# Sample states by head pair of four samples instead of by group of one sample, in the Mamba-2 part of a hybrid decoder step

## The reference, cut to what matters

```
new_state[b,h,p,n] = exp(sum of dt*a over the 4 tokens) * h0[b,h,p,n]
                     + sum_t  decay_to_end[t,h] * dt[t,h] * x[t,h,p] * B[t,g,n]
y_off[t,h,p]       = exp(acs[t,h]) * sum_n  C[t,g,n] * h0[b,h,p,n]
```

## Time and profile before

| | us |
|---|---|
| median of 3 runs | 2291.16 (2288.71 to 2292.43) |
| profiled execution | 2290.49 |
| its span | 2289.3 |
| TensorE busy | 2222.1 |
| sample states: first turn to the end of the turns in `carry` | 1308.18 to 1361.33 |

### The profile page before, as it was taken

One profiled execution on the slowest core, in us unless ns is written; L12 is line 12 of the kernel. 1 busy time (PEld: TensorE's weight loads), 2 busy tenths in 40 slices (PEclk: granted clock), 3 DMA queues, 4 the chain that ended last, 5 costly groups with the idle time before them and its releaser, 6 DMA issues.

```text
span 2289.3 us, 41851 instructions
## 1 busy us (share of the span) xinstructions
PE 2222.1 (97%) x16986; PEld 2161.8 (94%) x16986; DVE 1193.4 (52%) x1545; ACT 820.4 (36%) x798; POOL 162.5 (7%) x224
## 2 busy tenths in 40 slices
PE   6999999999999999999899899899999999999998
PEld 6999999999999999988787879899999999999997
DVE  5545445454455557556436656555544555445554
ACT  5333333332333343344353434433323333333333
POOL 2410000000000130100000402000000000000022
PEclk8999999999999999999999999999999999999999
DMA  8665565655656567656875465665566665666552
GB/s 197 171 166 158 162 176 161 168 155 163 177 158 169 145 160 208 186 168 190 268 227 174 126 176 154 166 168 160 164 167 166 166 164 159 172 166 166 158 156 95
DMA packets 696130, 386.51 MB, mean 169 GB/s; under 512 B 18216, under 2 KB 677836, under 8 KB 695192
## 3 DMA queue, kind: packets, MB, share of 16 engines
q1 hardware_dynamic: 691528, 378.79, 60.1%
q0 software_dynamic: 4112, 5.94, 1.0%
q10 hardware_dynamic: 384, 0.30, 0.0%
HBM read 373.86 MB, written 11.13 MB: 168 GB/s over the span
## 4 chain that ended last, share of the span: by engine, by line
PE 87%; DVE 5%; SPq 2%; ACT 2%; issue 2%; DMA 1%; POOL 0%; ACTq 0%; DVEq 0%; POOLq 0%
PE bank L785 28%; PE bank L787 27%; PE bank L786 27%; DVE wlo L1507 1%; SPq L476 1%; PE bank L810 1%; ACT whi L1192 1%; SPq L475 1%; PE bank L1067 1%; PE bank L983 0%; DVE lseg L1870 0%; DMA kpage<-cache_k 0%; PE bank L1074 0%; DVE xn_lo L1497 0%; PE bank L929 0%
## 5 line engine op out<-in xcount | busy, mean ns | idle before, releaser
L785 PE MATMUL bank<-xn_hi,whi 128*128 128x288 f32 x3536 | 1059.0, 299 | 29.5 <-DVE wlo L1507 11.5
L786 PE MATMUL bank<-xn_hi,wlo 128*128 128x288 f32 x3536 | 1050.5, 297 | 0.0
L787 PE MATMUL bank<-xn_lo,whi 128*128 128x288 f32 x3536 | 1046.8, 296 | 0.0
L1507 DVE TENSOR_TENSOR wlo<-wraw,whi 128x2048 fp32r<-128x2048 f32 (+3 forms) x341 | 726.4, 2130 | 401.4 <-ACT whi L1192 401.0
L1192 ACT CAST whi<-wraw 128x2048 fp32r<-128x2048 f32 (+3 forms) x341 | 604.8, 1775 | 748.9 <-PE bank L787 743.5
L785 PEld LDWEIGHTS bank<-xn_hi,whi 128*128 128x128 f32 x3536 | 670.1, 190 | 39.9 <-issue 20.5
L787 PEld LDWEIGHTS bank<-xn_lo,whi 128*128 128x128 f32 x3536 | 673.0, 190 | 0.0
L786 PEld LDWEIGHTS bank<-xn_hi,wlo 128*128 128x128 f32 x3536 | 671.3, 190 | 0.1
L786 PE MATMUL bank<-h_hi,wlo 128*128 128x288 f32 x1376 | 407.1, 296 | 0.0
L787 PE MATMUL bank<-h_lo,whi 128*128 128x288 f32 x1376 | 406.6, 296 | 0.0
L785 PE MATMUL bank<-h_hi,whi 128*128 128x288 f32 x1376 | 401.8, 292 | 0.0
(11 more groups left out here) (351 smaller groups left out, 1149.2 us busy)
## 6 DMA issues: line engine op xcount, KB each, us to landing
wraw<-ffn_w_gate SPq DMA_DIRECT2D x86, 1024.0 KB, 5.9
wraw<-ffn_w_up SPq DMA_DIRECT2D x86, 1024.0 KB, 5.8
wraw<-ffn_w_down SPq DMA_DIRECT2D x64, 960.0 KB, 5.5
wraw<-w_in SPq DMA_DIRECT2D x40, 1024.0 KB, 6.4
wraw<-ffn_w_down SPq DMA_DIRECT2D x32, 832.0 KB, 5.2
kpage<-cache_k SPq DMA_DIRECT2D x64, 256.0 KB, 3.0
vpages<-cache_v SPq DMA_DIRECT2D x64, 256.0 KB, 3.5
wraw<-w_out SPq DMA_DIRECT2D x64, 256.0 KB, 3.1
```

What stands on the lines that cost most here:

```text
L785: pe.matmul(out, hi, rhs_hi, start=k == 0, stop=False)
L786: pe.matmul(out, lo, rhs_hi, start=False, stop=False)
L787: return pe.matmul(out, hi, rhs_lo, start=False, stop=k == nk - 1)
L1507: dve.tensor_tensor(tile_ap(wlo, s, nk), tile_ap(wraw, (base + j) % LOADS, nk), tile_ap(whi, s, nk).bitcast(F32), ALU.subtract).then_inc(s ...
```

## The change

- A unit becomes one head pair c = u//2 of four samples b0 = 4*(u%2) to b0+3, [128, 4 samples, 128]. `h0_of` gives the new view of the states; the number of units, their size and the ring stay.
- The outer product of a unit is one product of 512 columns: weights `xsn` of the pair, moving operand `bexp` with B of the group copied for each of four samples and masked to that sample's tokens. `bexp` for all samples and both groups is made once, in `decay_x`, in two instructions; it lies in a part of `xn_hi` that is free then.
- The C products of a unit are four products of 128 columns, one for each sample, on the four column tiles of the array, in every unit. Each column tile (row group of 32 in PSUM) collects its samples' rows; two units of a pair accumulate.
- `carry` scales all 128 rows, and the eight turns become eight products with `stack` (four identities one above the other), which add the four row groups while turning.
- The scaled sample x lies at rows 32 to 63 (`SX`) of `xsn`, and `nat_e` must stand in all four row groups: `turn_copies` makes such copies with products against the identity on several column tiles.
- `bmask` is made on VectorE instead of GpSimd, at the start, with `stack`.

```diff
-    bexp = Plan(nc, AT["lseg"], A1)("bexp", [P, 4, 256])
+    bexp = Plan(nc, AT["xn_hi"] + 4 * 4 * N, AT["xn_lo"])("bexp", [2 * NS, 2, ND, P])
+    SX = slice(NS, 2 * NS)
...
-        return t[0, u // 2, 8 * (u % 2):8 * (u % 2) + 8].rearrange("(j e) p n -> (e p) j n", e=2)
+        return t[0, 4 * (u % 2):4 * (u % 2) + 4, u // 2 * 2:u // 2 * 2 + 2].rearrange("b e p n -> (e p) b n")
+
+    def copies(ap, n):
+        return ap.unsqueeze(1).to_broadcast([ap.shape[0], n, ap.shape[1]])
+
+    def copied_rows(b):
+        return P if b < 2 else 2 * NS
...
-        pool.memset(bmask[:], 1.0).then_inc(sem("pool_fill"), 1)
...
-        pool.affine_select(out=bmask[:], in_=bmask[:], compare_op=ALU.is_ge, fill=0.0, base=0, pattern=[[-NT, ND]],
-                           channel_multiplier=1).then_inc(sem("pool_fill"), 1)
...
-        pool.affine_select(out=bmask[:], in_=bmask[:], compare_op=ALU.is_ge, fill=0.0, base=NT - 1,
-                           pattern=[[NT, ND]], channel_multiplier=-1)
...
+            def turn_copies(out, src, many, n=P):
+
+                if many == 1:
+                    return turn(out, src, n)
+                for r in range(many):
+                    m = pe.matmul(out[r * NS:(r + 1) * NS, :], src, ident[0:n, 0:n], start=True, stop=True)
+                return m
...
-                            turn(to[0:rows_of(b), b * 144 + pl * 48:b * 144 + pl * 48 + 48], sc48[0:48, pl, toks(b)], 48)
-                    turn(to[0:NS, 432:480], e48[0:48, :], 48).then_inc(side_done("nat"), 1)
+                            src = sc48[0:48, pl, toks(b)]
+                            turn_copies(to[:, b * 144 + pl * 48:b * 144 + pl * 48 + 48], src, 1 if b < 2 else 2, 48)
+                    turn_copies(to[:, 432:480], e48[0:48, :], 4, 48).then_inc(side_done("nat"), 1)
...
-                            m = turn(to[0:rows_of(i), c * P:(c + 1) * P], xsT[:, 4 * half + c, toks(i)])
+                            src = xsT[:, 4 * half + c, toks(i)]
+                            m = turn_copies(to[:, c * P:(c + 1) * P], src, 1 if i < 2 else 2)
...
-                        b, g = (i - 1) // 2, (i - 1) % 2
-                        to = claim(pe, "up", i - 1)
-                        pe.wait_ge(sem("bexp_ready"), b + 1)
-                        for j in range(4):
-                            c = 4 * g + j
-                            m = pe.matmul(to[:, j * P:(j + 1) * P], xsn[0:NS, 2, c * P:(c + 1) * P],
-                                          bexp[0:NS, b % 4, g * ST:(g + 1) * ST], start=True, stop=True)
-                        m.then_inc(side_done("up", i - 1), 1)
-                        if g == 1:
-                            for q in range(2):
-                                copied(pe, "ht", 2 * b + q)
-                            for q in range(2):
-                                pe.matmul(bank[2 + q][NS * q:NS * (q + 1), :], cpad[:, q, b, :], h0t[:, q, :],
-                                          start=b == 0, stop=b == ND - 1).then_inc(sem("h0t_used"), 1)
+                        u = i - 1
+                        c, b0 = u // 2, 4 * (u % 2)
+                        to = claim(pe, "up", u)
+                        pe.wait_ge(sem("bexp_ready"), 2)
+                        pe.matmul(to[:, :], xsn[SX, 2, c * P:(c + 1) * P], bexp[SX, c // 4, b0:b0 + 4, :],
+                                  start=True, stop=True).then_inc(side_done("up", u), 1)
+                        copied(pe, "ht", u)
+                        for q in range(4):
+                            m = pe.matmul(bank[2 + c // 4][NS * q:NS * (q + 1), c % 4 * P:(c % 4 + 1) * P],
+                                          cpad[:, c // 4, b0 + q, :], h0t[:, u % 2, q * P:(q + 1) * P],
+                                          start=b0 == 0, stop=b0 > 0)
+                        m.then_inc(sem("h0t_used"), 1)
...
-                        m = turn(to[:, j * NS:(j + 1) * NS], ys[0:NS, j * P:(j + 1) * P], NS)
+                        m = pe.matmul(to[:, j * NS:(j + 1) * NS], ys[:, j * P:(j + 1) * P], stack[:], start=True, stop=True)
...
+        dve.tensor_reduce(stack[:], ident[:].rearrange("p (r t) -> p t r", t=NS), AX.X, ALU.add)
+        dve.tensor_reduce(bmask[SX, :], ident[SX, SX].rearrange("p (b t) -> p b t", t=NT), AX.X, ALU.add)
...
-                    for b in range(3):
-                        n = rows_of(b)
-                        xv = xsn[0:n, b, :].rearrange("p (h c) -> p h c", c=HD)
-                        m = dve.tensor_tensor(xv, xv, spread(nat[0:n, b, 96 + 32:96 + 48], HD), ALU.mult)
+                    for b, rows in ((0, slice(0, P)), (1, slice(0, P)), (2, SX)):
+                        xv = xsn[rows, b, :].rearrange("p (h c) -> p h c", c=HD)
+                        m = dve.tensor_tensor(xv, xv, spread(nat[rows, b, 96 + 32:96 + 48], HD), ALU.mult)
                     m.then_inc(sem("xw_ready"), 1)
+                    for g in range(2):
+                        dve.tensor_tensor(bexp[SX, g, :, :], copies(bnat[SX, 2, g * ST:(g + 1) * ST], ND),
+                                          spread(bmask[SX, :], ST), ALU.mult).then_inc(sem("bexp_ready"), 1)
                 elif what == "unit":
-                    if i % 2 == 0 and i < 2 * ND:
-                        b = i // 2
-                        if b >= 4:
-                            take(dve, "up", 2 * (b - 4) + 1)
-                        dve.tensor_scalar(bexp[0:NS, b % 4, :], bnat[0:NS, 2, :], bmask[:, b:b + 1], None, ALU.mult)\
-                            .then_inc(sem("bexp_ready"), 1)
...
-                                                         scalar=dec[:, 4 * g + j, b:b + 1], in1=src[:, cs],
+                                                         scalar=dec[:, u // 2, 4 * (u % 2) + j:4 * (u % 2) + j + 1],
+                                                         in1=src[:, cs],
...
-                        dve.tensor_tensor(ys[0:NS, g * 512:(g + 1) * 512].rearrange("p (h c) -> p h c", c=HD),
-                                          bank[2 + g][NS * g:NS * (g + 1), :].rearrange("p (h c) -> p h c", c=HD),
-                                          spread(nat_e[0:NS, 32 + 8 * g:40 + 8 * g], HD), ALU.mult).then_inc(sem("ys_ready"), 1)
+                        dve.tensor_tensor(ys[:, g * 512:(g + 1) * 512].rearrange("p (h c) -> p h c", c=HD),
+                                          bank[2 + g][:, :].rearrange("p (h c) -> p h c", c=HD),
+                                          spread(nat_e[:, 32 + 8 * g:40 + 8 * g], HD), ALU.mult).then_inc(sem("ys_ready"), 1)
```

More of the change, by code:

```diff
@@ L100, in build @@
     hot = fixed("hot", [P, H_SSD], F32R)
+    stack = fixed("stack", [P, NS])
+    bmask = fixed("bmask", [2 * NS, ND])
     mseg3 = fixed("mseg3", [P, 3 * P + NS])
@@ L578, in _ @@
         pool.memset(col[:], 0.0).then_inc(sem("pool_fill"), 1)
-        pool.wait_ge(sem("pool_fill"), 6)
+        pool.wait_ge(sem("pool_fill"), 5)
         for c in (0, 2):
@@ L585, in _ @@
                            channel_multiplier=1).then_inc(sem("pool_fill"), 1)
-        pool.affine_select(out=bmask[:], in_=bmask[:], compare_op=ALU.is_ge, fill=0.0, base=0, pattern=[[-NT, ND]],
-                           channel_multiplier=1).then_inc(sem("pool_fill"), 1)
         pool.affine_select(out=head_rows[:], in_=head_rows[:], compare_op=ALU.is_ge, fill=0.0, base=0, pattern=[[1, NS]],
                            channel_multiplier=-NT).then_inc(sem("pool_fill"), 1)
-        pool.wait_ge(sem("pool_fill"), 9)
+        pool.wait_ge(sem("pool_fill"), 7)
         pool.affine_select(out=head_rows[:], in_=head_rows[:], compare_op=ALU.is_ge, fill=0.0, base=NT - 1,
@@ L599, in _ @@
         pool.memset(col[0:72, 0:1], -1.0).then_inc(sem("pool_fill"), 1)
-        pool.wait_ge(sem("pool_fill"), 10)
+        pool.wait_ge(sem("pool_fill"), 8)
         pool.memset(col[SR, 0:1], 1.0).then_inc(sem("tables_ready"), 1)
@@ L1024, in mix_tensor @@
                     for c in range(2):
-                        m = turn(to[0:rows_of(i), c * P:(c + 1) * P], xsT[:, 8 + c, toks(i)])
+                        src = xsT[:, 8 + c, toks(i)]
+                        m = turn_copies(to[:, c * P:(c + 1) * P], src, 1 if i < 2 else 2)
                     m.then_inc(side_done("b", i), 1)
@@ L1728, in mix_vector @@
                     dve.tensor_copy(nat[:, 0:2, :].rearrange("p b c -> p (b c)"), src[:, 0:288])
-                    dve.tensor_copy(nat_e[0:NS, :], src[0:NS, 432:480])
-                    dve.tensor_copy(nat[0:NS, 2, :], src[0:NS, 288:432]).then_inc(side_read("nat"), 1)
+                    dve.tensor_copy(nat_e[:], src[:, 432:480])
+                    dve.tensor_copy(nat[0:2 * NS, 2, :], src[0:2 * NS, 288:432]).then_inc(side_read("nat"), 1)
                     src = take(dve, "dec")
@@ L1836, in mix_vector @@
                 elif what == "turn_x":
-                    n = rows_of(i)
+                    n = copied_rows(i)
                     for half in range(2):
@@ L1845, in mix_vector @@
```

(2 more changed lines are left out.)

2 lines of the change are left out of this document (removed).

## The result

The changed kernel takes 2292.99 us (median of 12 runs, 2291.18 to 2299.74) against 2289.2 (12 runs, 2284.2 to 2294.27): ratio 1.0022, interval 1.0013 to 1.0031. The difference of 3.8 us is small, but the whole interval lies above 1: the change made the kernel slower. The forecast was 0.8 us faster.

The account below looks back on a forecast made before the run. TensorE, busy for 97% of the span, bounds the kernel. Saved 4.4 us less 3.6 lost is 0.8 net: the profiled 2290.49 becomes 2289.7, as median of runs 2290.4; range 2286 to 2296, same verdict at 0.75.

Parts of the forecast that it names:

- the first one: Opening step: TensorE is busy for 97% of the span, so the question is which of its stretches the change touches.
- Rival 2: Old-state loads bind at three places with longest landing: 2293.7; with falls of TensorE's clock 2298.5, slower; chance 0.09.
- Outer product: Sample-state units: one 512-column product takes 0.97 us (bounds 0.85 to 0.98) instead of 1.085; 1.8 us saved.
- C products: Sample-state units: four 128-wide products on four column tiles take 0.35 us per unit (0.24 to 0.40); 1.6 us saved.
- rival 1: Four column tiles don't run at once when a unit brings one group: 9.4 us more, 2299.8, slower; chance 0.05.
- Wait for ScalarE: Sample-state units: TensorE's 0.26 us wait for ScalarE's copy of the turned state goes four times; 1.0 us saved.
- Old states: Late loads stall the turns of states 6, 10 and 14 by 0.4 us each, 1.2 in all; 0.9 lost.
- carry: Eight turns become eight products, 16 passes, taking 1.8 us in place of 0.5; 1.3 us lost (up to 1.65).
- The clock's one fall in the stage: Sample-state stage before the change: TensorE's clock fell once, around 1340; a mean of 0.97 means 1.6 us lost.
- rival 4: The one fall of TensorE's clock in the sample-state stage goes: 1.6 us faster, 2288.8; chance within the forecast's 0.75.
- Turns with copies and gates: Before `scores`, sample turns of x and B: 0.95 us lost (0 to 1.2); gate turns: 0.45 lost (0.2 to 0.6).

Follow-up runs that it names:

- a_pad96: Changed kernel with 96 unused bytes behind bmask, so h_hi and h_lo start 256 bytes later than in the kernel before: 2289.6 us, ratio 0.9996.
- a_out4: a_pad96 with the one 512 wide outer product of a unit put back to four of 128 columns: 2293.86 us (one run).
- a_fill: a_pad96 with output tiles from carry on moved one place forward, so a tile of products stands before carry: 2287.48 us, ratio 0.9995.
- b_pad160: Kernel before the change with 160 unused bytes behind hot, nothing else: 2295.62 us, ratio 1.0026.
- b_xn32: Kernel before the change with 32 unused bytes in front of xn_hi and 32 more behind hot: 2296.24 us, ratio 1.0025.
- a_xn96: Changed kernel with gaps of 224 bytes in front of xn_hi and 128 in front of xn_lo: 2280.35 us (6 runs), ratio 0.9966.
- a_w32: Changed kernel with 32 bytes in front of the split weights and 96 behind them: 2276.79 us (6 runs), ratio 0.9952.

## Why the prediction was wrong

The forecast, 2290.4 with same as the likeliest, missed: the kernel got slower by 3.8 us, and not a little faster. The range, 2286 to 2296, holds the 2292.99 all the same, and 3.8 is less than the 4.6 that the prediction took for the least that can be told. For the changed stages in sum the forecast is not refuted: `a_pad96` differs from before by -0.04%, the forecast by -0.03%. But the interval of `a_pad96` is 0.12% to either side, and the terms below are off in both directions, so that the agreement is in part luck.

**The step that failed** is the first one: "the question is which of its stretches the change touches", answered by the stages whose code changed. The two new tiles of the fixed region, 160 bytes, were costed only by what fills them. They also move every tile behind them, and so touch 4128 products of the down projections: a loss of 4.7 us, the largest single effect that the runs show. No rival had this. Rival 2's 2293.7 lies near the measured time, by another mechanism, and its mechanism was not there: no turn of an old state waits for its load in the changed kernel's trace.

The single terms, by their own names:

- **Outer product**: mis-sized. 1.05, not 0.97; outside my bounds (0.85 to 0.98). 16 x 0.035 = 0.6 saved, not 1.8. On top of the stream of 0.85 lie 0.20, not the 0.13 that the C products before the change had; why, no run shows.
- **C products**: 0.36, as forecast (0.35). Four tiles do run at once; rival 1 is out.
- **Wait for ScalarE**: gone for TensorE's products, as forecast.
- **Old states**: no wait in the changed kernel, 0.5 in `a_pad96`, 1.5 in `a_out4`. The forecast of 1.2 was too much as a rule: of the 12 traces with the changed stage 4 show no such wait, 7 one of 0.3 to 0.6 at state 6, and `a_out4` alone waits at the three turns that were forecast. Each trace's landings decide: from issue (1318.34) to the turn of state 6 (1322.01) there are 3.67, and by the view of the tile of old states in the stage loads land after (least, median, most):

```profile
DMA to landing us min/median/max: 3.0/3.2/5.0
```

- **`carry`**: mis-sized by the clock. The 16 passes take 1.78 at full clock (`a_fill`; forecast 1.8) but 3.41 behind the gap: 2.8 lost against the 0.57 of before, where 1.3 was forecast. Of the 13 other traces with such a gap (2.15, or 1.63 in the kernels without the change), 9 have the passes or turns of `carry` at that lower pace throughout, 3 in part, and the trace of before not at all. `b_pad160` and `b_xn32` take 0.96 for the turns, so a part of the 2.8 is a chance of the one trace of before. The products behind `carry` come every 0.24 for some more microseconds (0.62 from 1358 to 1362: about 1.5 lost), but so they do in all 14 traces with the gap, in that of before from 1362 on:

```profile
1360.00:1364.00 4.00, 3.25 (x22) 3.23 (x23) 2.65 (x6) 1.63 (x3) 0.00 (x0) 0.79 0.91 262
1364.00:1368.00 4.00, 4.00 (x27) 4.00 (x26) 2.15 (x4) 2.21 (x3) 0.00 (x0) 0.79 0.67 196
```

- **The clock's one fall in the stage**: gone, as rival 4 had it; in the changed kernel the granted clock is 1.00 from 1307 to 1352, against 0.80 and 0.77 in two windows of 4 us before, about 1.7 gained. With outer products 0.6, C products 1.5, ScalarE 1.0, loads 0.3 and `carry` -2.8 that gives 2.3; the stage shows 2.14. That 51.01 came out as 51.0 is therefore luck: against the terms of the prediction the outer products (1.2) and `carry` (1.5) gave less, the loads (1.2) and the clock (1.7) more, and these cancelled.
- **Turns with copies and gates**: from the first turn to `scores` 5.36 against 4.47 (forecast 0.95 lost, measured 0.89), and the gates 0.96 against 0.67 (forecast 0.45, measured 0.29). VectorE now waits for TensorE there, as said:

```profile
1232.49 1.25 PE L813 MATMUL bank<-ident,xsT 128*128 128x128 f32 x10
...
1235.54 2.38 PE L820 MATMUL bank<-ident,xsT 128*32 128x128 f32 x40
1236.65 0.68 DVE L1855 TENSOR_TENSOR xsn<-bank,nat 64x512 f32<-64x512 f32 x1 [0.32 <-PE bank L820]
...
1237.85 2.13 PE L1046 MATMUL bank<-xsT 128*128 128x256 f32 x12
```

**What stays open**: why a distance of 64 or 96 mod 128 is cheaper than 0 or 32, and why one good distance makes a whole triple cheap. The rows show durations, not what TensorE waits for inside a product. That weights and moving operand meet in the memory would fit a rule of distance, but no run shows it. Nor is it explained why `a_xn96` (0.9966) and `a_w32` (0.9952), with the same prices and, by the splits, the same time in the two SwiGLU blocks (-3.06 and -4.21, -3.04 and -4.21 against before), differ by 0.14% in their ratios; the intervals overlap. The kernel before with the distances of `a_w32` wasn't run; by its prices it should gain as much.

## What to carry to other kernels

When a change adds or resizes a tile in a hand-laid memory, list what lies behind it and compare the pace of the unchanged products, from start to start, first: a nanosecond in each of ten thousand products (11.3 us by the triples of `xn`) outweighs a whole rebuilt stage (2.1 here). Lay two traces side by side at an instruction that both have in the same order, and see where the offset grows, before explaining anything by the changed code; look at the same stretch in a third trace before calling a gain the change's. A local gain in front of a wait for another engine (`carry`, `a_fill`) counts only after the next wait has been looked at.

## What was not expected of the hardware

- The pace of these fp32r products of 288 columns depends on the distance between the starts of the moving operands and of the weights in SBUF: 396.5 to 402.9 ns per triple, 1.6%, over the distances tried, in steps of 32 bytes. The Trainium skill, "SBUF — State Buffer", section "SBUF: two separate sides", says of the engines' ports that TensorE never waits on anyone, and in its subsection "A bandwidth-pool intuition that's wrong (but worth ruling out)" gives weight loads a second, independent read port. Neither sentence speaks of where tiles lie, and a reader would not expect from them that it counts; here it does, and the measurement decides. Whether a port is what the products wait for, no run shows.
- With gaps of 32 and 96 bytes around the weights (`a_w32`) the changed kernel takes 0.9952 of the time before (0.9936 to 0.9968), 11.7 us by the medians; 3536 triples by 3.2 ns are 11.3.
- Behind 2.15 us without work TensorE ran the 16 passes of `carry` at a granted clock of 0.50 (3.41 us), behind 0.26 at 1.00 (1.78 us). Of the 11 traces of the changed kernel and its variants with the gap of 2.15, 8 have all the passes at the lower clock and 3 only the later ones.
